# Second gate of the mixer as half products of a two-by-two block scheme, in four sets of seven

## The reference

```
h1 = LN1(ALPHA*x  + 0.5*SwiGLU_1(x))
h2 = LN2(ALPHA*h1 + Mixer(h1))
y  = LN3(ALPHA*h2 + 0.5*SwiGLU_2(h2))
Mixer: z = h1 @ w_in -> u (pool branch), q, k, v, two gate vectors of 1024
  pool branch   pz   = group-wise pooled and scaled u
  attention     att  = sliding-window attention of q, k, v (with a softmax)
  merge         m    = sigmoid(gate_A) * (pz @ w_pool_out) + sigmoid(gate_B) * (att @ w_attn_out)
  out           m @ w_out
```

## Time and profile before

| | |
|---|---|
| median of 3 runs | 1072.14 us (1071.37 to 1072.96) |
| the profiled execution | 1070.73 us |
| its span, first to last instruction | 1068.9 us |
| outside the span | 1.83 us |
| mean granted TensorE clock | 0.994 of full speed |

### The profile page before, as it was taken

How to read it: one execution, slowest core, us unless ns; L and a number is a source line. 1 busy time by engine, 2 the same in 40 slices (tenths; PEclk the granted TensorE clock), 3 DMA queues, 4 the chain that set the end, 5 groups by cost and what they waited for, 6 DMA issues and landing times.

```text
span 1068.9 us, 20809 instructions
## 1 busy us (share of the span) xinstructions
PE 1041.0 (97%) x8177; PEld 1023.4 (96%) x8177; DVE 765.4 (72%) x1230; ACT 482.3 (45%) x849; POOL 231.5 (22%) x283
## 2 busy tenths in 40 slices
PE   8999999999999999999999999999999999999995
PEld 8899999999999989998899999989999999999995
DVE  6784799536996775987564576898578963689766
ACT  5453555314554353375452242655355531455424
POOL 2320223002311465000000005623012210221054
PEclk9999999999999999999999999999999999999998
DMA  9782577616754223221122351168357761575302
GB/s 329 168 224 84 144 186 202 171 60 150 186 131 149 77 96 105 70 70 40 50 85 75 99 175 54 50 128 203 109 136 170 189 173 59 129 179 147 119 1 84
DMA packets 77984, 135.17 MB, mean 126 GB/s; under 512 B 9208, under 2 KB 32056, under 8 KB 77864
## 3 DMA queue, kind: packets, MB, share of 16 engines
q1 hardware_dynamic: 58656, 87.45, 25.2%
q0 software_dynamic: 19232, 46.39, 20.3%
HBM read 131.32 MB, written 3.68 MB: 126 GB/s over the span
## 4 chain that ended last, share of the span: by engine, by line
PE 85%; DVE 6%; issue 3%; POOL 2%; DMA 2%; ACT 2%; SPq 0%; DVEq 0%; POOLq 0%; ACTq 0%
PE psum L1672 15%; PE psum L1674 14%; PE psum L1673 14%; PE psum L1746 13%; PE psum L1747 13%; PE psum L1748 13%; DMA sums<-in_ffn_up 1%; POOL p L688 1%; DVE ring_lo L1140 1%; PE psum L1882 1%; POOL fsum L682 1%; PE psum L1898 1%; DMA xin<-in_x 1%; DVE t_op L1183 1%; DVE stat L1326 1%
## 5 line engine op out<-in xcount | busy, mean ns | idle before, releaser
L1746 PE MATMUL psum<-t_op,ring_hi 128*128 128x272 f32 x640 | 184.3, 288 | 3.4 <-issue 1.8
L1748 PE MATMUL psum<-t_op,ring_lo 128*128 128x272 f32 x640 | 184.6, 288 | 0.0
L1747 PE MATMUL psum<-t_op,ring_hi 128*128 128x272 f32 x640 | 184.0, 287 | 0.0
L1133 DVE TENSOR_TENSOR ring_lo<-raw,ring_hi 128x1024 fp32r<-128x1024 f32 (+2 forms) x87 | 97.2, 1117 | 106.4 <-ACT ring_hi L816 106.3
L1672 PE MATMUL psum<-act_hi,ring_hi 128*128 128x272 f32 x512 | 150.5, 294 | 6.8 <-DVE act_lo L1347 2.8
L1674 PE MATMUL psum<-act_hi,ring_lo 128*128 128x272 f32 x512 | 148.7, 290 | 0.0
L1673 PE MATMUL psum<-act_lo,ring_hi 128*128 128x272 f32 x512 | 148.1, 289 | 0.0
L1672 PE MATMUL psum<-hid,ring_hi 128*128 128x272 f32 x512 | 147.4, 288 | 0.0
L1673 PE MATMUL psum<-hid,ring_hi 128*128 128x272 f32 x512 | 147.0, 287 | 0.0
L1674 PE MATMUL psum<-hid,ring_lo 128*128 128x272 f32 x512 | 146.8, 287 | 0.0
L1746 PE MATMUL psum<-act_hi,ring_hi 128*128 128x272 f32 x480 | 138.6, 289 | 1.9 <-DVE ring_lo L1140 1.9
(11 more groups left out here) (255 smaller groups left out, 2565.9 us busy)
## 6 DMA issues: line engine op xcount, KB each, us to landing
raw<-in_ffn_up SPq DMA_DIRECT2D x95, 256.0 KB, 3.3
sums<-in_ffn_up POOLq DMA_DIRECT2D x80, 256.0 KB, 4.5
sums_odd<-in_ffn_up POOLq DMA_DIRECT2D x80, 256.0 KB, 4.6
raw<-in_ffn_down SPq DMA_DIRECT2D x64, 256.0 KB, 3.0
raw<-in_mix_wide SPq DMA_DIRECT2D x52, 256.0 KB, 2.9
raw<-in_ffn_up SPq DMA_DIRECT2D x82, 128.0 KB, 4.0
raw<-in_ffn_down SPq DMA_DIRECT2D x32, 192.0 KB, 3.5
raw<-in_mix_proj SPq DMA_DIRECT2D x32, 128.0 KB, 2.2
```

The lines of the kernel that those rows point to most:

```text
L1133: dve.tensor_tensor(lo[:, 0:kn, :], raw[:, n % RAWS, 0:kn, :], hi[:, 0:kn, :], ALU.subtract) \
L1746: pe.matmul(o, w[0][:, k, :], x[0], start=k == 0, stop=False)
L1747: pe.matmul(o, w[0][:, k, :], x[1], start=False, stop=False)
L1748: ins = pe.matmul(o, w[1][:, k, :], x[0], start=False, stop=k == HK - 1)
```

## The change

The second gate and the attention's output product leave the unit loop, which now ends after unit 25 (`MIX1` = 26; it still runs two more steps, 26 and 27, for chunk 1). Behind it stands a late stage of four sets (`LATE`). A set makes two blocks of 128 columns of the second gate for both chunks from seven half products (four contraction tiles each, 12 matmuls) in the place of 8 x 8 tiles; then two blocks of the attention's output product ("row1", "row0", 24 matmuls each). DVE combines the seven results in the buffer `held`, ACT takes the sigmoid there, DVE multiplies and adds `m1`, ACT rounds to `m_hi`, DVE subtracts to `m_lo`, all for both chunks at once.

Four sums of quarters of h1 are needed (128 x 1088 values each). POOL makes them (`gate_sum`), each waiting for a place in the attention: the first two for the end of unit 17, the next for Sb, the last for T3. ACT and DVE split them into parts (`split_gate_term`) at the end of steps 21, 22 and 23, and the last one behind the loop. Sums of weight quarters come from POOL's accumulating DMAs and from DVE, as in the SwiGLU stages. Buffers move in memory, the scratch of POOL's DMA queue is halved, and the first two `w_out` units are issued up to their sixth tile before their last two tiles.

The diff, cut to its core:

```diff
-MIX1 = 42
+MIX1 = 26
...
+GATES = 4
+LATE = [(j, n) for j in range(GATES) for n in (1, 2, 5, 6, 7, 4, 3, "row1", "row0")]
+LATE_LOADS = 4 * GATES
+NHALF = 2 * SLOTS
+GATE0 = 18
...
+        def gate_term_home(i):
+
+            if i == 0:
+                return act_hi[:, 0:HK, tok(1)], act_lo[:, 0:HK, tok(1)]
+            w = (None, gate_t2, gate_t3, gate_t4)[i]
+            return w[:, 1], w[:, 0]
+
+        def gate_sum(i):
+
+            return gate_sum1[:, 0:HK, tok(1)] if i == 0 else (None, gate_sum2, gate_sum3, gate_sum4)[i][:, :, :]
...
+        GATE_SPLIT = {21: 0, 22: 1, 23: 2}
+        GATE_READY = {0: 2, 1: 3, 2: 4, 3: 3}
+        GATE_LO = {0: 1, 1: 2, 2: 3, 3: 4}
...
+            def gate_sums(j):
+
+                gates = a["mix_wide"].rearrange("u p k n -> p u k n")
+                a11 = gates[:, GATE0 + 2 * j, 0:HK]
+                a21, a22 = gates[:, GATE0 + 2 * j + 1, 0:HK], gates[:, GATE0 + 2 * j + 1, HK:KD]
+                for name in (5, 7):
+                    if j:
+                        pool.wait_ge(late_lo, LATE.index((j - 1, name)) + 1)
+                        if name == 5:
+                            pool.wait_ge(late_sum, 2 * j - 1)
+                    else:
+                        pool.wait_ge(op_lo, PRODS)
+                        pool.wait_ge(sum_done, 2 * PAIRS)
+                    pool.dma_start(sums_odd[:, (name == 7) + 0], a21).then_inc(late_base[name], 16)
+                for name, quarter in ((5, a22), (7, a11)):
+                    pool.wait_ge(late_base[name], 16 * (j + 1))
+                    pool.dma_start(sums_odd[:, (name == 7) + 0], quarter, accum_op=ALU.add).then_inc(late_in[name], 16)
+
+            def quarter_of(h, c):
+                return y[:, h * HK:(h + 1) * HK, tok(c)]
+
+            gate_sums(0)
+            pool.wait_ge(mm_done[1], MIX_BASE + U_PA)
+            pool.tensor_tensor(gate_sum(0), quarter_of(0, 0), quarter_of(0, 1), ALU.subtract).then_inc(gate_term, 1)
+            pool.wait_ge(gate_term, 1)
+            pool.tensor_tensor(gate_sum(1), gate_sum(0), quarter_of(1, 1), ALU.add).then_inc(gate_term, 1)
+            pool.wait_ge(gate_term, 2)
+            pool.wait_ge(att_mm, written("Sb"))
+            pool.wait_ge(side_stored, 16 * SIDE_STORES)
+            pool.tensor_tensor(gate_sum(3), gate_sum(1), quarter_of(1, 0), ALU.subtract).then_inc(gate_term, 1)
+            pool.wait_ge(att_mm, written("T3"))
+            pool.tensor_tensor(gate_sum(2), quarter_of(1, 1), quarter_of(0, 1), ALU.subtract).then_inc(gate_term, 1)
+            for j in range(1, GATES):
+                gate_sums(j)
             all_norm_sums(1)
...
+            def split_gate_term(i):
+
+                act.wait_ge(gate_term, GATE_READY[i])
+                if i == 3:
+                    act.wait_ge(mm_done[1], WO_BASE)
+                act.activation(gate_term_home(i)[0], gate_sum(i), ACT.Copy, scale=-1.0 if i == 1 else 1.0) \
+                    .then_inc(gate_term_hi, 1)
+
+            def split_late(h):
+
+                j, name = LATE[h]
+                if h < NHALF:
+                    act.wait_ge(mm_done[1], WO_BASE - SLOTS + h // 2 + 1)
+                else:
+                    act.wait_ge(late_mm, h - NHALF + 1)
...
+                    act.wait_ge(late_in[name], 16 * (j + 1))
+                elif name in (6, 3):
+                    act.wait_ge(late_sum, 2 * j + {6: 1, 3: 2}[name])
+                else:
+                    n = late_load(j, {1: 0, 2: 0, 4: 1, "row1": 2, "row0": 3}[name])
+                    act.wait_ge(raw_in[n % RAWS], loaded(n))
...
+                act.wait_ge(m_full, 2 * j + 2 - row)
+                e = 4 * (j % 2) + 2 * row
...
+                        m_row(before[0], before[1] == "row1")
+                    if name == 1:
+                        act.wait_ge(late_mm, i + 1)
+                        if j:
+                            act.wait_ge(late_comb, 4 * j - 3)
+                        act.activation(tmp_a[:, 0, :], psum[:, 0, 0:C], ACT.Copy).then_inc(late_copied, 1)
+                    if i + NHALF < len(LATE):
...
                     epilogue(s - LAG, 1)
-                    split(MIX_BASE + s + 2)
+                    if s + 2 < MIX1:
+                        split(MIX_BASE + s + 2)
+                    else:
+                        split_late(2 * (s + 2 - MIX1))
+                        split_late(2 * (s + 2 - MIX1) + 1)
                 beside(s)
+                if s in GATE_SPLIT:
+                    split_gate_term(GATE_SPLIT[s])
+            split_gate_term(3)
+            late_stage()
...
+            def split_gate_term(i):
+
+                hi, lo = gate_term_home(i)
+                dve.wait_ge(gate_term_hi, GATE_LO[i])
+                if i == 1:
+                    ins = dve.scalar_tensor_tensor(out=lo, in0=gate_sum(i), scalar=-1.0, in1=hi, op0=ALU.mult,
+                                                   op1=ALU.subtract)
+                else:
+                    ins = dve.tensor_tensor(lo, gate_sum(i), hi, ALU.subtract)
...
+            def split_late(h):
+
+                dve.wait_ge(late_hi, h + 1)
+                hi, lo = late_home(h)
+                dve.tensor_tensor(lo, late_source(h), hi, ALU.subtract).then_inc(late_lo, 1)
...
+                j, name = LATE[h]
+                if name == 6:
+                    f0 = late_load(j, 0)
+                    dve.wait_ge(raw_in[f0 % RAWS], loaded(f0))
+                    dve.wait_ge(late_in[5], 16 * (j + 1))
+                    dve.wait_ge(late_lo, LATE.index((j, 1)) + 1)
+                    ins = dve.tensor_tensor(late_source(h), sums_odd[:, 0], late_source(h), ALU.add)
+                else:
+                    dve.wait_ge(late_sum, 2 * j + 1)
+                    dve.wait_ge(late_lo, LATE.index((j, 2)) + 1)
+                    ins = dve.tensor_tensor(late_source(h), late_source(h), late_source(LATE.index((j, 6))), ALU.add)
...
             for s in range(MIX1 + LAG):
                 if s < MIX1:
...
                 beside(s)
+                if s in GATE_SPLIT:
+                    split_gate_term(GATE_SPLIT[s])
+            split_gate_term(3)
+            late_stage()
...
+            def late_product(i):
+
...
+                    if name in (5, 6, 7, 4):
+                        pe.wait_ge(gate_term_lo, {5: 1, 6: 2, 7: 3, 4: 4}[name])
+                elif name == 1:
+                    pe.wait_ge(late_copied, j)
+                elif name in (2, 6, 5, 7):
+                    pe.wait_ge(late_mul, 2 * j - (name in (2, 6)))
                 else:
-                    if m == U_GB + 1:
-
-                        pe.wait_ge(att_free, freed("PVs" if c else "PV2"))
-                    part(u, c, NG, of(att_hi, att_lo, c))
+                    pe.wait_ge(late_comb, 4 * j - (name != 3))
+                pe.wait_ge(late_lo, i + 1)
+                w = late_home(i)
+                bank = {1: 0, 2: 1, 6: 2, 4: 3, 5: 4, 7: 5, 3: 6}[name]
+                for k in range(HK):
+                    if name in (1, 2, 3):
+                        x = [t[:, k if name == 1 else HK + k, tok(name == 3)] for t in (act_hi, act_lo)]
+                    else:
+                        x = [t[:, k, :] for t in gate_term_home({5: 0, 6: 1, 7: 2, 4: 3}[name])]
+                    o = psum[:, bank, 0:C]
+                    pe.matmul(o, w[0][:, k, :], x[0], start=k == 0, stop=False)
+                    pe.matmul(o, w[0][:, k, :], x[1], start=False, stop=False)
+                    ins = pe.matmul(o, w[1][:, k, :], x[0], start=False, stop=k == HK - 1)
+                ins.then_inc(late_mm, 1)
+
...
+                for c in range(2):
+                    if c == 0:
+                        pe.wait_ge(late_comb, 4 * j + (1 if name == "row1" else 3))
+                    o = psum[:, (1 if name == "row1" else 4) + c, 0:C]
+                    for k in range(NG):
+                        pe.matmul(o, w[0][:, k, :], att_hi[:, k, tok(c)], start=k == 0, stop=False)
+                        pe.matmul(o, w[0][:, k, :], att_lo[:, k, tok(c)], start=False, stop=False)
+                        ins = pe.matmul(o, w[1][:, k, :], att_hi[:, k, tok(c)], start=False, stop=k == NG - 1)
+                ins.then_inc(late_mm, 1)
...
+            for i, (j, name) in enumerate(LATE):
+                if name in ("row1", "row0"):
+                    attended_row(i)
+                else:
+                    late_product(i)
+
+            def m_wait(k):
+                pe.wait_ge(m_ready, k // 2 * 2 + 2)
+
+            for s in range(2):
+                part(WO_BASE + s, 0, KD, of(m_hi, m_lo, 0), ready=m_wait, hi=KD - 2)
+            for s in range(2):
+                part(WO_BASE + s, 0, KD, of(m_hi, m_lo, 0), ready=m_wait, lo=KD - 2)
+            for s, c in WO_ORDER[2:]:
+                part(WO_BASE + s, c, KD, of(m_hi, m_lo, c),
...
-    nc = bacc.Bacc("TRN2", target_bir_lowering=False, num_devices=1, dynamic_dma_scratch_size=8192)
```

(56 more changed lines are left out.)

225 lines of the change are left out of this document (173 added, 52 removed).

## The result

The changed kernel takes 1075.63 us (median of 8 runs, 1073.50 to 1077.09) where the kernel before, run beside it, takes 1071.32 (8 runs): a ratio of 1.0035, with a 95% interval of 1.0025 to 1.0045. It is slower, by 4.3 us. The forecast was 1072.0, at most 1074.8.

A forecast was written before the change was run, and what follows sets the result against it. TensorE was taken to bound the kernel, carrying 85% of the chain that ended last. 6.0 us of matmuls go and waits of 2.4, 1.8 and 1.7 come, -0.1 us, giving a median of 1072.0 us, range 1069.2 to 1074.8.

The forecast's parts named there:

- What goes: Second gate: 336 matmuls in place of 384, so 48 at 0.125 us, 6.0 us, go from TensorE.
- Waits 1, 2 and 3: In the attention, TensorE waits at unit 21, unit 24 and Ta: 2.4, 1.8 and 1.7 us.
- Wait 1: At unit 21: POOL's first two sums, 2.0 us each, delay DVE's division and unit 21's weight; TensorE waits 2.4 us.
- the unknown of this step: At unit 21: whether DVE's multiplications wait out POOL's second sum; taken that they do, 2.4 us, otherwise 0.7.
- The sum: Whole kernel: -6.0 + 2.4 + 1.8 + 1.7 = -0.1 us, forecast as a median of 1072.0 us.
- The late stage: The second gate's sets of 132 matmuls, 16.5 us, with DVE busy 88%: no wait, costed at nothing.
- The lead of eight half slots: Late stage: weights are split eight half slots, about 14 us, ahead of TensorE, which covers DVE's work.
- (d): Late stage: POOL's quarter sums come too late, +6 us with landings of 9 each, 1078 us; chance 0.06.
- (a): Attention: POOL's sums cost DVE little, the waits at unit 24 and Ta stay, 1069.6 to 1070.3 us; chance 0.25.
- (b): Whole kernel: the full gain, 1066.1 us, needing some 3 us of slack at the division; chance 0.05.
- (c): Attention: slower POOL sums make the wait at unit 21 3.6 us, 1073.2 us in all; chance 0.15.
- The unseen wait in the late stage: Late stage: a wait not seen (ACT's copy of product 1, the sigmoid's table), 2 to 4 us, 1074 to 1076; chance 0.08.

The follow-up runs named there:

- `tile_ahead`: `both_moved` with the first weight tile of late sets 2 and 4 loaded a whole set earlier, nothing left out: 1065.91 us, ratio 0.9948 to the kernel before.
- `sums_again`: The kernel before with only GpSimd's first two sums added, into a buffer nothing reads, run once more for its profile: 1078.09 us (one run).
- `both_again`: `both_moved` once more, unchanged, run beside `tile_ahead`: 1066.94 us, ratio 0.9957 to the kernel before.
- `both_moved`: The changed kernel with the edits of `sums_later` and `splits_moved` together: 1068.14 us, ratio 0.9968 to the kernel before.
- `splits_moved`: The changed kernel with ACT's and DVE's parts of the activation sums made at other steps: 1071.28 us, ratio 1.0001 to the kernel before.
- `sums_later`: The changed kernel with GpSimd's first two sums held back until DVE has made unit 21's low part: 1071.29 us, ratio 1.0003 to the kernel before.

## Why the prediction was wrong

- **What goes**: right. 8129 matmuls for 8177, and once the waits are gone `tile_ahead` shows 5.4 of the 6.0 us.
- **Waits 1, 2 and 3**: the mechanism was right. By the starts of TensorE they are 3.2, 1.7 and 1.7 us, 6.6 where 2.4 + 1.8 + 1.7 = 5.9 stood. Wait 1 was mis-sized because a sum of 1088 columns takes 2.50 us and not 2.0: the scaled rows had given 2.1 to 2.6, and I went below them. (The Trainium skill has 4.5 us for 2048 columns on GpSimd, in "GPSIMD Engine Reference", section 3.1; scaled, an estimate of 2.4, which the measured 2.50 bears out.) That the multiplications wait out a sum, the unknown of this step, was right: 2.47 us for 0.34. (This agrees with the rule that the prediction took from the Trainium skill, "SBUF — State Buffer", section "Who interferes with whom", for tensor_scalar.)
- **The sum**: this is the step that failed. It entered each wait at its delay alone and kept every other matmul at 0.125 us, since the granted clock is 1.00 in the rows it came from the earlier trace rows. Behind wait 1 the clock fell to 0.50, in both profiles of the changed kernel and in the three profiles of other kernels with that wait, for 1.7 us more (3.4 in `sums_again`); an average run loses 2.3 us more to the clock than before. -6.0 + 6.6 + 2.3 is 2.9. (The Trainium skill describes waits of TensorE that are followed by slow matmuls in "TensorE: Matmul & The Clock Gate", section "HAM oscillation — how this bites in real kernels"; the trace agrees, here behind single waits of 1.65 to 3.05 us, and the prediction should have weighed it as a rival.)
- **The late stage**, costed at nothing: 0.7 and 1.2 us in the two profiles. The lead of eight half slots hid DVE's work, as argued, but what set it back was not looked for, the first weight tile's load. Where TensorE comes to the stage earlier, it costs 1.6 to 3.0 us (`both_again`, `both_moved`, `splits_moved`, `sums_later`: 67.6, 67.9, 68.1, 69.0 for 66.0). So the three waits in the attention seem to have hidden a part of this; no run shows it by itself.
- With these terms the sum is 3.6 to 4.1 us; measured are 4.3 (2.7 to 4.8) and 4.6 (3.5 to 6.2). The middle lies 0.2 to 1.0 us higher, within the intervals.
- **Rivals**: (d), GpSimd's quarter sums late, did not come: no wait on them stands in front of TensorE. Nor did (a) and (b): the sums delay DVE in full, and only `tile_ahead`, without the waits, comes near the full gain. (c) had wait 1 at 3.6; 3.2 is between that and the forecast. The unseen wait in the late stage came about as priced, in other versions than this.

## What to carry to other kernels

Work given to an idle engine is not free where a busy one has to wait for it: here 5 us of GpSimd's additions held up the division that stood ahead of the weight that TensorE was waiting for, and the same additions 3.3 us later delayed nothing that TensorE waited for. Price a wait of TensorE as the delay of its next start plus what the clock may take behind it: here 3.05 us of idle time cost 3.2 + 1.7 = 4.9. And after a wait is removed, look at the next stage again, since the wait may have been hiding a load that is late there.

## What the hardware showed that was not expected

- The granted clock fell in the middle of a stage in which TensorE was otherwise busy: behind a single wait of 3.05 us at unit 21, and in `sums_later` behind one of 1.78 us; behind those of 1.53 and 1.44 us in the changed kernel it did not. Counted over all thirteen profiles, from 20 to 1050 us: all ten waits of 1.99 to 3.05 us have a drop behind them, of thirty waits of 1.59 to 1.90 us seven have one, and no drop stands anywhere else. So the length of a wait does not settle it alone: one of 1.78 to 1.79 us near 717 is in twelve of the profiles, five times with a drop.
- Where such drops come differs between profiles of one kernel: `both_moved` has none, and `both_again`, the same kernel, one of 1.7 us.
- A DVE instruction of 8 columns waits out GpSimd's running sum like one of 256: 1.94 us for 0.16, and 2.47 for 0.34.
